# Two-block model, input projection: the first mean square on ScalarE, weights asked for first, key columns projected once, the gate by rows

## The reference, cut to what matters

```python
def rms_norm(x, g):
    xf = x.astype(jnp.float32)
    y = xf * lax.rsqrt(jnp.mean(xf * xf, axis=-1, keepdims=True) + NORM_EPS)
    return (y * g.astype(jnp.float32)).astype(x.dtype)
...
z = rms_norm(h, pre_mix_norm[i]) @ w_in[i]
z_rw, z_nsa, z_s5 = _split(z, (RWKV_COLS, NSA_COLS, S5_W))
...
q, kc, vc, ks, vs, kw, vw, gl = _split(z, NSA_SPLITS)      # 384, six times 128, 18 columns
k_cmp = compress(kc, pe_k, w1_k, w2_k)
v_cmp = compress(vc, pe_v, w1_v, w2_v)
...
g_blocks = jax.nn.sigmoid(gl)                              # the gate of three attention branches
```

## Time and profile before

| | us |
|---|---|
| median of three runs | 1455.54 |
| their range | 1453.73 to 1458.12 |
| the profiled execution | 1459.26 |
| its span in the profile | 1457.3 |
| TensorE busy | 1362.4 (93%) |
| VectorE, ScalarE, GpSimd busy | 562.4, 619.2, 833.8 |

### The profile page before, as it was taken

One profiled execution on the slowest core, in us unless ns is written; L12 is line 12 of the kernel. 1 busy time (PEld: TensorE's weight loads), 2 busy tenths in 40 slices (PEclk: granted clock), 3 DMA queues, 4 the chain that ended last, 5 costly groups with the idle time before them and its releaser, 6 DMA issues.

```text
span 1457.3 us, 26522 instructions
## 1 busy us (share of the span) xinstructions
PE 1362.4 (93%) x11138; PEld 1277.3 (88%) x11138; DVE 562.4 (39%) x1241; ACT 619.2 (42%) x925; POOL 833.8 (57%) x419
## 2 busy tenths in 40 slices
PE   6989798979899999989999999999999987999998
PEld 5987355868899999989999999989999877999997
DVE  4645867651255472322433302132233242333301
ACT  3532153223465554544444434544544343554431
POOL 5872430022388878545688775845655443688771
PEclk9998798996899999989999999999999999899998
DMA  7945898330455555434455554443636683455550
GB/s 219 207 123 188 301 383 312 120 112 4 134 171 185 175 180 179 140 108 149 141 177 193 166 188 146 140 132 91 186 91 216 192 286 102 158 178 192 167 159 30
DMA packets 246323, 244.96 MB, mean 168 GB/s; under 512 B 25652, under 2 KB 215230, under 8 KB 246206
## 3 DMA queue, kind: packets, MB, share of 16 engines
q1 hardware_dynamic: 245715, 243.10, 52.2%
q10 hardware_dynamic: 491, 0.17, 0.1%
HBM read 242.20 MB, written 1.05 MB: 167 GB/s over the span
## 4 chain that ended last, share of the span: by engine, by line
PE 83%; DVE 6%; issue 2%; ACT 2%; DMA 2%; POOL 0%; DVEq 0%; ACTq 0%
PE banks L533 82%; DVE arena L1584 2%; DMA ring<-in_attn_w_o_dram 1%; DVE arena L1591 1%; ACT arena L2291 1%; DMA ring<-in_ffn_w_up_dram 1%; PE banks L543 0%; DVE banks L1591 0%; ACT ring_hi L2291 0%; DVE ring_lo L1584 0%; DVE arena L1772 0%; PE banks L818 0%; DVE arena L1588 0%; DVE hn L1591 0%; PE banks L941 0%
## 5 line engine op out<-in xcount | busy, mean ns | idle before, releaser
L1535 POOL TENSOR_TENSOR ring_lo<-ring,ring_hi 128x2048 fp32r<-128x2048 f32 (+1 forms) x176 | 718.7, 4096 | 510.4 <-ACT ring_hi L2291 510.0
L533 PE MATMUL banks<-hn_hi,ring_lo 128*128 128x256 f32 x1888 | 539.1, 289 | 0.0
L533 PE MATMUL banks<-hn_hi,ring_hi 128*128 128x256 f32 x1696 | 484.4, 290 | 7.6 <-ACT hn_hi L2291 7.6
L533 PE MATMUL banks<-hn_lo,ring_hi 128*128 128x256 f32 x1696 | 445.0, 283 | 0.0
L2291 ACT ACTIVATE ring_hi<-ring 128x2048 fp32r<-128x2048 f32 (+1 forms) x176 | 299.7, 1704 | 179.7 <-PE banks L533 131.0
L533 PEld LDWEIGHTS banks<-hn_hi,ring_lo 128*128 128x128 f32 x1888 | 375.2, 199 | 0.0
L533 PEld LDWEIGHTS banks<-hn_hi,ring_hi 128*128 128x128 f32 x1696 | 335.0, 198 | 9.6 <-issue 9.4
L533 PEld LDWEIGHTS banks<-hn_lo,ring_hi 128*128 128x128 f32 x1696 | 310.9, 193 | 0.1
L2291 ACT ACTIVATE arena<-banks 128x256 f32<-128x256 f32 (+5 forms) x229 | 90.3, 411 | 319.1 <-PE banks L533 265.4
L533 PEld LDWEIGHTS banks<-arena 64*128 64x128 f32 (+4 forms) x1282 | 122.7, 188 | 72.4 <-issue 52.3
L533 PE MATMUL banks<-arena 128*64 128x128 f32 (+9 forms) x1282 | 150.4, 314 | 32.1 <-issue 13.2
(11 more groups left out here) (236 smaller groups left out, 1706.0 us busy)
## 6 DMA issues: line engine op xcount, KB each, us to landing
ring<-in_ada_w_dram SPq DMA_DIRECT2D x48, 1024.0 KB, 8.3
ring<-in_ffn_w_up_dram SPq DMA_DIRECT2D x44, 1024.0 KB, 5.2
ring<-in_w_up_dram SPq DMA_DIRECT2D x22, 1024.0 KB, 5.1
ring<-in_ffn_w_down_dram SPq DMA_DIRECT2D x16, 1024.0 KB, 5.4
ring<-in_w_kv_dram SPq DMA_DIRECT2D x15, 1024.0 KB, 5.4
ring<-in_w_kv_dram SPq DMA_DIRECT2D x18, 512.0 KB, 3.9
ring<-in_attn_w_q_dram SPq DMA_DIRECT2D x18, 512.0 KB, 3.9
ring<-in_w_in_dram SPq DMA_DIRECT2D x8, 1024.0 KB, 12.1
```

The lines of the kernel that those rows point to most:

```text
L533: return nc.tensor.matmul(o, l, r, start=start, stop=stop, **k)
L1535: led.emit(g.tensor_tensor(low, raw, high.bitcast(F32), ALU.subtract), sem("lo_ready"))
```

## The change

1. ScalarE loads the table of square and root ahead of its issues. When x has landed, it squares the two row blocks of `xtok` with a sum along the row (`accum_out`), and takes the root: the mean square needs neither TensorE nor the turned x. ScalarE, not VectorE, copies the fourth turned piece.
2. SyncE asks for weight chunk 0 directly behind x. The rows of `soon` come after it, the token features p and all rows of `later` after chunk 1; ScalarE issues none of `later`.
3. The low part of chunk 0 is made on GpSimd (`first_lo`), between its mask selections. The others stay on VectorE, the one of chunk 2 now ahead of the S5 constants, those of the RWKV tiles behind every second tile, and the one of the first key chunk ahead of the S5 input matrices.
4. Two key chunks instead of four, each 64-column group once: `kc` and `kd` are two tiles each. ScalarE's copies write a half tile to either half of the partitions.
5. The gate is projected with the 18 columns as the weight and x moving (`gT`), goes through tanh by rows and is turned by TensorE after `u`.

```diff
-        for i, (c0, c1) in enumerate(((KC_COL, KC_COL + HD), (VC_COL, VC_COL + HD), (KS_COL, KS_COL + HD),
-                                      (KW_COL, KW_COL + HD))):
-            chunk_src["keys", i] = [kmaj(w_in, c, c + HD) for c in (c0, c0, c1, c1)]
-        early = [("in", i) for i in range(8)] + [("keys", i) for i in range(4)] + [("gate", 0), ("u", 0)]
+        chunk_src["keys", 0] = [kmaj(w_in, KC_COL, KS_COL)]
+        chunk_src["keys", 1] = [kmaj(w_in, KS_COL, VS_COL), kmaj(w_in, KW_COL, VW_COL)]
+        early = [("in", i) for i in range(8)] + [("keys", 0), ("keys", 1), ("gate", 0), ("u", 0)]
...
-            pe.wait_ge(sem("mean_ready"), 1)
-            mean_square(0, hn)
...
             for x, nm in enumerate(("kc", "kd")):
-                for i in range(4):
-                    split_tile((nm, i), ("keys", 2 * x + i // 2), 128 * (i % 2), xz)
-            split_rows(("gtok",), [(slice(s * 18, s * 18 + 18), slice(s * P, s * P + P)) for s in range(2)],
-                       ("gate", 0), xz)
+                for i in range(2):
+                    split_tile((nm, i), ("keys", x), 128 * i, xz)
+            split_tile(("gT",), ("gate", 0), 0, xz, 18)
             for i in range(2):
                 split_tile(("u", i), ("u", 0), 128 * i, xz)
+            copied(("gT",))
+            turn(("gtok",), [gate_rows[:, s * P:s * P + P] for s in range(2)])
...
             for n, key in enumerate(order):
+                if n == 1:
+                    sp.wait_ge(sem("stage_clear"), 2)
+                    stage_rows(sp, soon[0::2], sem("soon_in"))
+                if n == 2:
+                    sp.dma_start(ptok, a["p"][0, 0].rearrange("(s p) d -> p s d", p=P)).then_inc(sem("ple_in"), 16)
+                    stage_rows(sp, later, sem("later_in"))
...
+            raw, low, high = chunk_flat(early[0])
+            pool.wait_ge(sem("early_hi"), 1)
+            led.emit(g.tensor_tensor(low, raw, high.bitcast(F32), ALU.subtract), sem("first_lo"))
...
+            act_.wait_ge(setup_in, 16)
+            for s in range(2):
+                af(hn[:, 4 * s:4 * s + 4, :].rearrange("p a b -> p (a b)"), xtok[:, s, :], ACT.Square, scale=1.0 / 32,
+                   accum_out=rs[:, s:s + 1])
+            settle()
+            af(rs[:, 0:2], rs[:, 0:2], ACT.Sqrt, sem("first_root"), bias=eps_col)
```

More of the change, by code:

```diff
@@ L513, in chunk @@
                     begun.add(key)
-                    if key in early:
-                        pe.wait_ge(sem("early_lo"), early.index(key) + 1)
+                    if key == early[0]:
+                        pe.wait_ge(sem("first_lo"), 1)
+                    elif key in early:
+                        pe.wait_ge(sem("early_lo"), early.index(key))
                     elif key in split:
@@ L563, in three_passes, with split_tile @@
                 return mm(o, w_lo, x_hi, start=False, stop=stop)
-            def split_tile(job, key, c0, x):
+            def split_tile(job, key, c0, x, m=P):
                 b = opened(job)
@@ L569, in split_tile @@
                 for k in range(KT):
-                    last = three_passes(b[:, 0:T], [v[:, k, c0:c0 + P] for v in w], [v[:, k, :] for v in x],
+                    last = three_passes(b[0:m, 0:T], [v[:, k, c0:c0 + m] for v in w], [v[:, k, :] for v in x],
                                         k == 0, k == KT - 1)
@@ L606, in mean_square_of @@
                     if k % 2 == 0 or k == KT - 1:
-                        pe.wait_ge(sem("squares"), 5 * (i - (i > 4)) + (1, 1, 2, 2, 3, 3, 4, 5)[k])
+                        pe.wait_ge(sem("squares"), 5 * (i - 1 - (i > 4)) + (1, 1, 2, 2, 3, 3, 4, 5)[k])
                     for s in range(2):
@@ L1638, in scaled_parts @@
                 return wide, x
-            for j in range(4):
+            for j in range(2):
                 b = take(("xT", j))
@@ L1647, in early_low @@
                 tt(low, raw, high.bitcast(F32), SUB, sem("early_lo"))
-            early_low(0)
-            placed(("ms", 0))
+            dve.wait_ge(sem("first_root"), 1)
             rec(rs[:, 2:4], rs[:, 0:2], sem("rs_small"))
+            b = take(("xT", 2))
+            copy(h[:, 4:6, :], shaped(b, 2, T), *freed(("xT", 2)))
             b = take(("par", 0))
@@ L1740, in _ @@
                        signal=sem("b_ready") if ri and bb else None)
-            for c in range(8, len(early)):
+            for c in range(9, len(early)):
                 early_low(c)
-            placed(("gtok",))
-            ts(gate[:, :, :], gate[:, :, :], 0.5, MUL, 0.5, ADD)
+            b = take(("gtok",))
+            ts(gate[:, :, :].rearrange("p a b -> p (a b)"), b[:, 0:36], 0.5, MUL, 0.5, ADD, *freed(("gtok",)))
             b = take(("bT",))
@@ L2374, in early_high @@
                 af(high, raw, ACT.Identity, sem("early_hi"))
-            stage_rows(act_, later[1::2], sem("later_in"))
-            act_.dma_start(dt_rows[0:8, :], a["s5_log_dt"].rearrange("l (j g) -> (l j) g", g=2)).then_inc(sem("later_in"), 16)
             early_high(0)
+            high_parts(0, 0, hn_hi)
             early_high(1)
-            root(0)
-            high_parts(0, 0, hn_hi)
+            act_.wait_ge(sem("derived"), 1)
+            early_high(2)
             af(cond[:, :], cols("c", 8), ACT.Tanh, sem("cond_tanh"), scale=0.5)
@@ L2405, in kc_ @@
                 b = take(("kc", i))
-                af(kcs[0:64, i, :], b[0:64, 0:T])
-                af(kcs[64:128, i, 0:T - 1], b[64:128, 1:T], ACT.Identity, *freed(("kc", i)))
+                for g in range(2):
+                    group = b[64 * g:64 * g + 64, :]
+                    af(kcs[0:64, 2 * i + g, :], group[:, 0:T])
+                    af(kcs[64:128, 2 * i + g, 0:T - 1], group[:, 1:T], ACT.Identity,
+                       *(freed(("kc", i)) if g else (None, None)))
             def kd_(i):
                 b = take(("kd", i))
-                af(kd[:, i, :], b[:, 0:T], ACT.Identity, *freed(("kd", i)))
+                for g in range(2):
+                    for x in range(2):
+                        af(kd[64 * x:64 * x + 64, 2 * i + g, :], b[64 * g:64 * g + 64, 0:T], ACT.Identity,
+                           *(freed(("kd", i)) if g == x == 1 else (None, None)))
             def u_(i):
```

35 lines of the change are left out of this document (19 added, 16 removed).

## The result

The changed kernel took 1437.1 us in the median of its first four runs against 1454.6 before, a ratio of 0.9885 (0.9861 to 0.9909). So it is 17 to 20 us faster, where 26.5 were forecast: inside the range, at its upper end. The profiled execution took 1436.47 us for a span of 1434.4, 22.9 less than the 1457.3 of the one before.

The account below looks back on a forecast made before the run. The input projection was taken as bound by TensorE, with stalls, and its start by chunk 0's arrival. Start, keys, gate and u summed to 27.2 us earlier, less 0.5 for banks: 26.5 us, median 1429, range 1421 to 1438.

## What to carry over

When an edit removes or adds a user of a rotating resource (PSUM banks here), every later place that waits for a fixed member of the rotation has to be looked up, to the end of the program: ask who its last user is before and after. Work that is removed uncovers the chain it hid, so look for the next work without a condition to put there (u before the gate: 6.5 us by medians, 3.9 to 7.8 by the first S5 pass). Time the same code twice before taking stage lengths from it: two executions differed by 3 to 4 us in the front third. A wait put down to "issue" can be a bank: compare the release on the other engine before blaming the code.

## What was new of the hardware

The same code can differ by 3 to 4 us in its first tenth from one execution to the next, and most of that is granted clock. The changed kernel had its first S5 pass at 104.23 and 100.33; a chunk of 48 matmuls behind a stall of 2.6 to 2.9 us ran once at granted clock 0.78 (7.50 us) and once at 1.00 (5.84), which is 1.7 of the 3.9. The front third of the kernel before had it at 127.51 and 124.19, and there 100 matmuls with no stall among them took 16.0 us at 0.68 and 12.8 at 0.87.
